# Second tile's out products by column halves, a router that reads the raw sum, and a first gather in fp32

## The reference

```
x = x + gt1 * (merged @ w_out)
h = rms_norm(x, g_ffn) * (1 + sc2) + sh2          # modulate
logits = h @ w_router + b_router                  # 256 x 32
top_vals, top_idx = top_k(logits, 4); top_w = softmax(top_vals)
for each expert e, for the tokens that chose it:
    gu  = h[tok] @ w_gu[e] + b_gu[e]              # 1024 x 2048
    act = (clip(up) + 1) * min(gate, 7) * sigmoid(1.702 * gate)
    x[tok] += gt2 * top_w * (act @ w_down[e] + b_down[e])
x = rms_norm(x, g_final)
```

## Time and profile before

| | us |
|---|---|
| median of three runs | 1226.66 |
| the profiled execution | 1225.74 |
| its span | 1223.6 |
| TensorE busy (share of the span) | 1145.6 (94%) |
| VectorE busy | 472.9 (39%) |
| ScalarE busy | 126.9 (10%) |
| GpSimd busy | 123.7 (10%) |
| DMA: 459.97 MB | mean 376 GB/s |

### The profile page before, as it was taken

The page is one execution under the profiler, slowest core; times in us unless marked ns, Lnnn a source line. Parts: engine busy times, 40 slices in busy tenths (PEclk is TensorE's granted clock), DMA queues, the critical chain, the costliest instruction groups (busy, mean ns, idle before and its releaser), DMA issues.

```text
span 1223.6 us, 18139 instructions
## 1 busy us (share of the span) xinstructions
PE 1145.6 (94%) x7036; PEld 495.6 (41%) x7036; DVE 472.9 (39%) x831; ACT 126.9 (10%) x255; POOL 123.7 (10%) x146
## 2 busy tenths in 40 slices
PE   5989989986999999999999999999999999999996
PEld 4766668743333333333333333333333333333332
DVE  6778988525223322222222222333222222222223
ACT  3111213132000000000000000000000000000002
POOL 2676760011000000000000000000000000000000
PEclk9989999997999999999999999999999999999998
DMA  9983339993999999999999999999999999999995
GB/s 332 334 306 104 104 107 408 412 389 155 376 422 420 423 421 423 421 423 421 422 422 422 422 407 423 421 422 422 421 422 422 422 422 422 421 422 422 422 421 213
DMA packets 82276, 459.97 MB, mean 376 GB/s; under 512 B 13564, under 2 KB 13800, under 8 KB 31048
## 3 DMA queue, kind: packets, MB, share of 16 engines
q1 hardware_dynamic: 80680, 458.50, 92.0%
q10 hardware_dynamic: 1568, 1.08, 0.3%
HBM read 458.51 MB, written 1.05 MB: 376 GB/s over the span
## 4 chain that ended last, share of the span: by engine, by line
PE 56%; DMA 22%; DVE 9%; SPq 9%; issue 2%; ACT 1%; POOL 1%; DVEq 0%
PE ps L879 22%; PE ps L920 13%; DMA zone<-in_w_gu 11%; DMA ring<-in_w_down 9%; SPq L362 6%; PE ps L862 4%; PE ps L804 3%; PE ps L520 2%; PE ps L774 2%; PE ps L901 2%; SPq L367 2%; PE ps L871 1%; DMA ring<-in_w_glu 1%; PE ps L723 1%; PE ps L517 1%
## 5 line engine op out<-in xcount | busy, mean ns | idle before, releaser
L920 PE MATMUL ps<-ring,tmp 128*64 128x512 f32 x1024 | 230.5, 597 | 17.0 <-ACT tmp L1095 9.4
L879 PE MATMUL ps<-ring,zone 128*64 128x512 f32 x1024 | 235.8, 601 | 7.9 <-DMA ring<-in_w_gu 7.1
L879 PE MATMUL ps<-zone 128*64 128x512 f32 x896 | 205.2, 597 | 2.6 <-DMA zone<-in_w_gu 2.2
L1552 DVE TENSOR_TENSOR x_tok<-x_tok,ps 128x512 f32<-128x512 f32 x128 | 82.1, 682 | 264.3 <-PE ps L862 264.3
L879 PEld LDWEIGHTS ps<-ring,zone 128*64 128x64 f32 x1024 | 68.9, 137 | 168.1 <-issue 132.7
L920 PEld LDWEIGHTS ps<-ring,tmp 128*64 128x64 f32 x1024 | 71.6, 137 | 153.8 <-issue 136.3
L879 PEld LDWEIGHTS ps<-zone 128*64 128x64 f32 x896 | 60.7, 137 | 141.1 <-issue 128.5
L520 PE MATMUL ps<-hT,ring 128*128 128x256 f32 x448 | 101.3, 382 | 2.4 <-DVE hT L1256 2.4
L1565 DVE TENSOR_SCALAR hT<-ps 128x512 f32<-128x512 f32 x32 | 22.1, 692 | 200.7 <-PE ps L879 200.7
L1092 ACT ACTIVATE hT<-hT 128x512 f32<-128x512 f32 x32 | 20.2, 631 | 762.9 <-DVE hT L1565 762.9
L1546 DVE TENSOR_TENSOR tmp<-ps,zone 128x512 f32<-128x512 f32 x32 | 22.1, 692 | 185.0 <-PE ps L920 185.0
(11 more groups left out here) (284 smaller groups left out, 887.6 us busy)
## 6 DMA issues: line engine op xcount, KB each, us to landing
ring<-in_w_gu SPq DMA_DIRECT2D x128, 1024.0 KB, 25.9
ring<-in_w_down SPq DMA_DIRECT2D x128, 1024.0 KB, 22.2
zone<-in_w_gu SPq DMA_DIRECT2D x112, 1024.0 KB, 24.6
ring<-in_w_ada SPq DMA_DIRECT2D x24, 1024.0 KB, 10.7
ring<-in_w_in SPq DMA_DIRECT2D x16, 1024.0 KB, 14.4
xs<-in_w_gu SPq DMA_DIRECT2D x16, 1024.0 KB, 23.6
ring<-in_w_glu SPq DMA_DIRECT2D x4, 1024.0 KB, 16.9
ring<-in_w_out SPq DMA_DIRECT2D x4, 1024.0 KB, 16.3
```

The lines of the kernel that those rows point to most:

```text
L879: last = mm(ps[CAP * h:CAP * h + CAP, b, :], hg[:, j, :], w[:, 0, D * b + 512 * h:D * b + 512 * h + 512], start=False, stop=(j == GU_PIECE ...
L920: last = mm(ps[CAP * h:CAP * h + CAP, 3, :], actT[:, k % 4, k // 4, :], wk[:, 512 * h:512 * h + 512], start=False, stop=(j == DN_PIECES - ...
L1552: V.tensor_tensor(x_tok[:, t, 512 * h:512 * h + 512], x_tok[:, t, 512 * h:512 * h + 512], ps[:, 6 + h, :], ALU.add).then_inc(S["comb_add"], 1)
```

## The change

It is written in the same style, by hand, on all engines:

- The products of tile 1 with `w_out` come by column halves: all four pieces for columns 0 to 511, then all four for the others; a piece counts as used at its second half. VectorE adds each half to `x_tok` by itself.
- The router works on `x_tok` as it is: transposes are taken of `x_tok`, `wr` is multiplied once by the scale (`wr2`), the part of the shift is a product of its own (`router_shift`) that goes into `brt`, and 1/rms multiplies the logits afterwards.
- Sums for positions are made for each tile when its choice is there. The first gather takes tile 0 by its three bf16 parts early, and tile 1 at the end by eight fp32 matmuls from `xn_tok`; it lands in two banks, so that half of item 0's columns are modulated while the rest is made.
- The splitting into bf16 parts moves from GpSimd to VectorE and ScalarE; that of tile 1 comes after item 0 has begun.
- Banks and semaphores are laid out anew to fit. The five small DMAs stand where they stood.

```diff
+            def router_shift():
+                pe.wait_ge(S["late_in"], 80)
+                for k in range(KD):
+                    last = mm(ps[:, 3, 0:EXPERTS], mod[:, SH2 + k:SH2 + k + 1].to_broadcast([P, P]), wr[:, k, :], ...)
...
+            last.then_inc(S["out_up"], 1)
+            pe.wait_ge(S["row_sb"], 1)
+            router_shift()
+            for h in range(2):
                 for n in range(4):
+                    if (h, n) == (0, 1):
+                        gate_row(1)
+                    if (h, n) == (0, 2):
+                        pe.wait_ge(S["x1"], 1)
+                        pe.wait_ge(S["ya_set"], 2)
+                        router_columns(0, range(KD))
+                    if (h, n) == (1, 0):
+                        pe.wait_ge(S["h2_sb"], 1)
+                        pe.wait_ge(S["xn2"], 2)
+                        router(0, range(KD))
+                    if (h, n) == (1, 2):
...
+                        position_sums(tri, 0, 0, True, True)
+                        position_sums(ones, 0, 1, True, False).then_inc(S["pos_up"], 1)
+                    if (h, n) == (1, 3):
+                        pe.wait_ge(S["x1"], 2)
+                        router_columns(1, range(4))
...
+                        last = mm(ps[:, 6 + h, :], mergedT[:, k, P:T], w[:, kk, 512 * h:512 * h + 512], ...)
+                    if h == 1:
                         last.then_inc(w_used, 1)
...
+            for f in range(KD):
+                for c in range(3):
+                    mm(ps[:, 2 + f // 4, ...], xpart[:, c, 0, P * f:P * f + P], pick[:, 0, :], ...)
+            pe.wait_ge(S["h2_sb"], 2)
+            router(1, range(4))
+            pe.wait_ge(S["x1"], 3)
+            router_columns(1, range(4, KD))
+            pe.wait_ge(S["h2_sb"], 3)
+            pe.wait_ge(S["xn2"], 3)
+            router(1, range(4, KD))
...
+            for f in range(KD):
+                last = mm(ps[:, 2 + f // 4, ...], xn_tok[:, 1, P * f:P * f + P], pick32, ...)
...
-                pool.wait_ge(S["xh_set"], i + 1)
-                nc.gpsimd.tensor_tensor(xn_tok[:, i, :], xn_tok[:, i, :], xpart[:, 0, i], ALU.subtract)...
-                pool.wait_ge(S["xm_set"], i + 1)
-                nc.gpsimd.tensor_tensor(xpart[:, 2, i], xn_tok[:, i, :], xpart[:, 1, i], ALU.subtract)...
...
             modulation(2)
+            dve.wait_ge(S["late_in"], 80)
+            V.tensor_tensor(wr2, wr, scale2[:, :]..., ALU.mult).then_inc(S["xn2"], 1)
+            V.tensor_copy(hot[:, 0, 0:EXPERTS], cst[:, C_ID32:C_ID32 + EXPERTS]).then_inc(S["pos_sb"], 1)
...
+            expert_of(0)
+            dve.wait_ge(S["row_sb"], 1)
+            dve.wait_ge(S["out_up"], 1)
+            add_rows_of(0, 0, D, ps[:, 4:6, :]...)
+            dve.wait_ge(S["logit_up"], 1)
+            link(V.tensor_tensor(brt[:, :], ps[:, 3, 0:EXPERTS], brt[:, :], ALU.add))
...
+            chosen(0)
+            dve.wait_ge(S["out_up"], 2)
+            add_rows_of(1, 0, 512, ps[:, 6, :])
...
+            dve.wait_ge(w_used, USED)
+            add_rows_of(1, 512, 512, ps[:, 7, :])
...
+            inverse(1)
+            chosen(1)
+            counted(1)
+            V.tensor_scalar(pick32, slots, posI[:, 1, 0:1], None, ALU.is_equal).then_inc(S["pick_set"], 1)
...
+            first_modulated(0)
+            first_modulated(1)
```

More of the change, by code:

```diff
@@ L190, in build @@
     hotb = ptmp[:, CAP:2 * CAP]
+    pick32 = ptmp[:, 2 * CAP:3 * CAP]
+    wr2 = ptmp[:, 256:512].rearrange("p (k e) -> p k e", k=KD)
     gfin = xn_tok[:, 0, :]
@@ L730, in _, with router_columns @@
                     gate_row(0)
[L732 to L737, removed]
-                last.then_inc(S["x2T_up"], 1)
[L740 to L745, removed]
+            def router_columns(i, ks):
+                for k in ks:
+                    last = nc.tensor.transpose(x2T_bank(i, k), x_tok[:, i, P * k:P * k + P], ident)
+                last.then_inc(S["x2T_up"], 1)
@@ L753, in _ @@
-            for i in range(TT):
-                if i == 1:
-                    pe.wait_ge(S["row_sb"], 1)
-                for n in range(4):
-                    w = slot(place["out", n], 2)
[L758 to L770, removed]
+                if ks[-1] == KD - 1:
+                    last.then_inc(S["logit_up"], 1)
@@ new lines, in _ @@
+            for n in range(4):
+                w = slot(take("out", n), 2)
+                if n == 0:
+                    pe.wait_ge(S["ya_set"], 1)
+                pe.wait_ge(S["merged"], 1 if n < 2 else 2)
+                if n == 2:
+                    modulation_products(2)
+                if n == 3:
+                    modulation_columns(2)
+                for kk in range(2):
+                    k = 2 * n + kk
+                    for h in range(2):
+                        last = mm(ps[:, 4 + h, :], mergedT[:, k, 0:P], w[:, kk, 512 * h:512 * h + 512],
+                                  start=(k == 0), stop=(k == KD - 1))
@@ L771, in _ @@
                     for kk in range(2):
                         k = 2 * n + kk
[L773 to L776, removed]
+                        last = mm(ps[:, 6 + h, :], mergedT[:, k, P:T], w[:, kk, 512 * h:512 * h + 512],
+                                  start=(k == 0), stop=(k == KD - 1))
@@ L777, in _ @@
+                    if h == 1:
                         last.then_inc(w_used, 1)
-                if i == 0:
+                if h == 0:
                     last.then_inc(S["out_up"], 1)
[L780 to L785, removed]
-            pe.wait_ge(S["sel_set"], TT)
[L787 to L792, removed]
+            pe.wait_ge(S["pick_half"], 1)
@@ L867, in item @@
                 pe.wait_ge(S["hotb_set"], i + 1)
+                if first:
+                    pe.wait_ge(S["late_in"], 80)
                 for h in range(2):
@@ L892, in item @@
                 pe.wait_ge(S["pick_set"], i + 2)
+                if first:
+                    pe.wait_ge(S["x_split"], TT)
                 gather()
```

197 lines of the change are left out of this document (130 added, 67 removed).

## The result

The changed kernel takes **1239.24 us** (median of 4 runs, 1236.42 to 1244.14), the kernel before 1226.02 beside it (4 runs); the ratio is 1.0106, 95% interval [1.0063, 1.0148]. So it is slower, and by more than I said: the forecast was 1232.1, the upper end of the range 1238.5. The profiled execution took 1236.42 us, with a span of 1234.6 us, which is 11.0 us more than before.

What follows compares the result with a forecast made beforehand. Item 0's start was taken to set the end: 265.0 + 21.8 + 10.1 = 296.9 us against 291.48, 5.4 later, so 1231.1 us profiled and a median of 1232.1 us; range 1228.5 to 1238.5.

Steps and rivals of the forecast that it cites:

- What bounds the kernel: Experts: DMA engines are full from 300 us, so each microsecond of item 0's start moves the end by one.
- L: Time when all five small inputs have landed: 264.3 to 266.0 us, taken as 265.0; bounds 262.5 and 270.4.
- The small inputs stay slow: Rival on the small DMAs: they land only at 270.4 us, giving 1237.5 us; 12%.
- no wait bites: Rival: small inputs complete near 250 us, item 0 starts 10.9 us earlier, 1215.8 us; 10%.
- The wait: TensorE before `router_shift` and VectorE before `wr2`, both free at about 250.2 us, wait for the small inputs; 15 us.
- GpSimd's leaving, the choices, the additions: Before item 0: GpSimd's leaving gains some 3 us; tile 1's choice takes 2.1 us, the last half's addition 1.4.
- at most 0.4: Tail: most that the 1.8 us fp32 gather costs over the spared bf16 half, put at 1.4 us.
- It has been idle for 15 us, so it starts at half clock: TensorE after the wait: half clock during `router_shift`, 3.1 us, by which time full clock is back.
- L to last product: TensorE from the small inputs' landing to tile 1's last product: 21.8 us, ending at 286.8 us.
- The tail: From tile 1's last product to item 0's start: 10.1 us, including 0.5 for handovers.
- my 12% rival: Clock falls in the tail, from L + 25: gather, counts and bias products cost 3.4 us again, 1235.5 us; 12%.
- the 1.5 in my sum: Cost in us of half clock after TensorE's 15 us pause before L.

Runs made afterwards that it cites:

- run 4: Kernel before with only the two waits for the small inputs moved ahead of tile 1's products and tile 0's addition: 1241.13 us, ratio 1.0147.
- run 8: Changed kernel with small inputs issued early (about 205 us) and three filler matmuls in the tail: 1213.51 us, ratio 0.9894.
- run 9: Changed kernel, small inputs still late, with 17 filler matmuls in the 15 us pause and three in the tail: 1230.52 us, ratio 1.0031.
- run 5: Changed kernel with 17 filler matmuls on TensorE between tile 0's products and the wait for the small inputs: 1237.1 us, ratio 1.0093.
- run 7: Repeat, beside the unedited changed kernel, of the changed kernel with 17 filler matmuls in the pause: 1236.38 us, ratio 1.0086.
- run 6: Changed kernel once more, unedited, as base in the same session: 1237.27 us, ratio 1.0091.
- run 12: Changed kernel, TensorE's wait in the same place, but `router_shift` issued behind two blocks of 512-column products and the gate row: 1234.19 us, ratio 1.0064.
- run 1: Changed kernel with the five small DMAs issued at about 208 us instead of 239: 1218.07 us, ratio 0.9947.
- run 2: Kernel before with the five small DMAs issued early, at about 205 us: 1225.47 us, ratio 1.0007.
- run 10: Run 8 with bias-row DMAs issued at 127 us and the router's weights and bias at 223 us: 1218.6 us, ratio 0.9921.
- run 3: Changed kernel, `router_shift` moved ahead of tile 0's router and VectorE's scaling behind tile 0's addition: 1227.19 us, ratio 1.0026.

## Why the prediction was wrong

By its own steps:

- **What bounds the kernel: right.** Each microsecond of item 0's start is found again at the end. But the edge is not item 0's first product; it is the use of its third piece (`xs`), 5.55 us later at full clock.
- **L: right in kind, 0.2 us under its range.** Forecast 264.3 to 266.0, found 264.1: `b_down` lands 21.2 us after its issue, where it took 26.8 in the earlier trace rows. Of the 0.9 us that it is ahead of my 265.0, 0.8 are a mixer that ended earlier in this execution (`b_down` is issued at 242.8 us, before at 243.6). "The small inputs stay slow" and "no wait bites" fall with it.
- **The wait: right in place and size.** 14.88 us on TensorE, 17.85 on VectorE. Run 4 puts it at 16.4 us of time by itself, with half clock behind it.
- **GpSimd's leaving, the choices, the additions: right.** The tail at full clock takes 10.1 us in runs 8 and 9, to the tenth what I had worked out, with the gather at 1.89 us for my 1.8. One comparison in it was wrong, without weight in the sum: the 1.4 us for half of the bf16 gather were read at half clock. At full clock this half takes 0.86 us (24 records in run 8), so the fp32 gather costs 1.0 us more than it and not "at most 0.4".
- **The failing step: "It has been idle for 15 us, so it starts at half clock", with 3.1 us for `router_shift`, "by which time the clock is back".** Here the step took 3.6 us, and the clock wasn't back: it came 8.9 us after L, so that the following products and the gate row ran at half as well. L to last product was 24.9 us for the forecast 21.8. Filled (runs 5, 7, 9) it is 20.6. I had read a return within 3 us off one place of one execution and taken it for this one. Other work stood there, and at that very place run 4 had it after 8.6 us. Why the clock took 8.9 us here is open.
- **The tail: my 12% rival was the case.** "Against: the longest gap here is about 2.5 us" was no protection: the grant fell during a gap of 2.38 us. That is 2.7 us up to item 0, near the 3.4 I had given it. What the rival lacked is what comes behind it: the clock stays down for item 0's first pieces too, 2.65 us more.

The sum, from 1231.1 us for the profiled execution: L -0.9, half clock behind the wait +3.1, half clock in the tail +2.7, the same in item 0's first pieces +2.65, and -2.0 from the `xs` issue to the end. That gives 1236.65; it took 1236.42. Run 9 takes all three clock terms away at once and is 6.7 us faster than run 6, whose own trace has 7.6 us of them, so they are shown together; in the pause alone the trace shows it (runs 5 and 12) and the pair of medians of runs 6 and 7 does not.

The Trainium skill, "TensorE: Matmul & The Clock Gate", section "Part 1: The HAM clock gate", says that a pause puts the array at half of 2.4 GHz and steady work brings it back. The trace agrees in kind. What this cost here was 4.3 us behind the wait (24.9 against 20.6), 2.7 in the tail and 2.65 in item 0, 9.7 us in all, for the 1.5 in my sum.

Why the median came out at 1239.24 and in run 6 at 1237.27 is not settled; 4 and 6 runs don't tell them apart. Open too is the start of the mixer: at 68 to 74 us, ahead of everything edited, the profiled executions lie up to 6 us apart, behind a wait of TensorE for ScalarE's `zone` of 3.0 to 6.5 us. Runs 1, 2 and 10 had it late. Since each such microsecond reaches the end, spans of single executions are compared here only from L or from the last product on.

## What to carry to other kernels

When a wait moves forward in an engine's program, price three things: the pause, the time at the lower clock behind it, and the same for the next pause; here they were 15, 4 and 5 us. Ask first whether the awaited transfer can be issued earlier: 30 us earlier for 0.5 MB made this loss into a gain. If the wait must stay, put work that does not need it ahead of it (run 3). And don't take the time until the clock is back from a single place in a trace: here it was 3 to 9 us.

## What the runs showed of the hardware

- With the same pause of 14.8 to 14.9 us, the granted clock was full 2.8 and 3.1 us after work resumed where products with `w_out` came first (runs 12 and 4), and 8.9 and 6.2 us after where `router_shift` did (the changed kernel and run 6). In all four TensorE reads as busy without a gap. Behind a pause of 1.11 us, with the same gather first, it was full 3.0, 3.1 and 8.6 us after work resumed (the kernel before, runs 2 and 4). So what comes first doesn't explain it alone.
- In the changed kernel the clock fell at 293.5 us, 1.1 us into a gap of 2.38 us that followed others of 0.61 and 0.22 between small matmuls, with 20 us of full clock before it.
- Matmuls whose result nobody reads paid for themselves: three in the tail took the place of half a clock (1218.07 against 1213.51 us, different sessions).
- 16 records of the fp32 gather (weights 128x128, 64 columns) take 1.89 us at full and 3.65 at half clock; half of the bf16 gather that it replaces takes 0.86 at full clock (24 records in run 8), and took 1.4 in the earlier trace rows, nearly all of it at half clock.
- Small DMAs on ScalarE's queue landed 15.2 to 16.5 us after their issue where they were issued from 208 us on, and 21 to 27 us from 239 us on, beside the same stream of 1 MB pieces.
